# Keys of four sequences multiplied beside the prompt's attention, from early queries, and the other four's spread over the loop

## The reference, cut to what matters

```python
q, k, v, logf, u = project(x, w_in, b_f)                  # D 1024, 8 heads of 64
attn = fox_prompt(q, k, v, logf)                          # 1024 rows, causal, with a decay bias
pool = pool_mix(u_ext, 0, w_pool, pool_scale)
x1   = layer_norm(ALPHA * x + concat(attn, pool) @ w_o)
y    = layer_norm(ALPHA * x1 + (silu(x1 @ w_gate) * (x1 @ w_up)) @ w_down)   # DFF 2816
# the eight sequences: the same, with
s = einsum('bqhd,bkhd->bhqk', q, k_all) * HEAD_DIM ** -0.5 + (F[P:] - F)      # k_all: 4096 cached rows + 1
p = softmax(s);  out = einsum('bhqk,bkhd->bqhd', p, v_all)
```

## Time and profile before

| what | value |
|---|---|
| median of 3 runs | 1494.49 us (1493.03 to 1495.39) |
| profiled execution | 1488.73 us, its span 1486.6 us |
| PE busy | 1371.5 us (92%) |
| DVE busy | 735.6 us (49%) |
| POOL busy | 551.5 us (37%) |
| DMA | 252.91 MB, mean 170 GB/s |
| granted clock of TensorE, mean | 0.960 of full speed |

### The profile page before, as it was taken

The page is one execution under the profiler, slowest core; times in us unless marked ns, Lnnn a source line. Parts: engine busy times, 40 slices in busy tenths (PEclk is TensorE's granted clock), DMA queues, the critical chain, the costliest instruction groups (busy, mean ns, idle before and its releaser), DMA issues.

```text
span 1486.6 us, 21226 instructions
## 1 busy us (share of the span) xinstructions
PE 1371.5 (92%) x7585; PEld 1089.1 (73%) x7585; DVE 735.6 (49%) x1078; ACT 354.7 (24%) x514; POOL 551.5 (37%) x267
## 2 busy tenths in 40 slices
PE   7899999999886989999999999999999999998774
PEld 5898888989686967777767777776777777756421
DVE  4745454453678764455363635564645452325702
ACT  4534353532410232020201120212111112112300
POOL 1110000022135329466457374764665732120500
PEclk9999999999898999999999999999999999999756
DMA  7312011010366437857567577575784863433895
GB/s 254 110 58 67 34 33 68 30 50 1 121 216 200 127 100 243 263 165 236 191 216 246 165 250 249 194 243 169 227 268 154 255 212 113 142 136 127 313 348 212
DMA packets 103176, 252.91 MB, mean 170 GB/s; under 512 B 12576, under 2 KB 13985, under 8 KB 97688
## 3 DMA queue, kind: packets, MB, share of 16 engines
q1 hardware_dynamic: 99776, 240.68, 49.0%
q0 software_dynamic: 3296, 10.88, 2.1%
HBM read 241.89 MB, written 9.86 MB: 169 GB/s over the span
## 4 chain that ended last, share of the span: by engine, by line
PE 79%; DVE 10%; DMA 6%; issue 3%; ACT 2%; SPq 0%; DVEq 0%; ACTq 0%
PE PSM L1271 30%; PE PSM L1289 16%; PE PSM L1041 9%; DMA AR<-ws 4%; PE PSM L1311 4%; PE PSM L1107 4%; PE PSM L1219 4%; PE PSM L1054 3%; PE PSM L1093 2%; PE PSM L1250 1%; DMA WR<-xT 1%; PE PSM L1373 1%; PE PSM L1360 1%; DVE WL L1434 1%; PE PSM L1123 1%
## 5 line engine op out<-in xcount | busy, mean ns | idle before, releaser
L692 POOL TENSOR_TENSOR AR<-AR,QB 128x1024 f32<-128x1024 f32 x128 | 319.0, 2516 | 64.8 <-DMA AR<-cache_k 49.8
L699 POOL TENSOR_TENSOR WL<-WR,WH 128x1024 fp32r<-128x1024 f32 x55 | 133.4, 2426 | 360.7 <-ACT WH L909 360.7
L1271 PE MATMUL PSM<-XH,WH 128*128 128x512 f32 x672 | 215.8, 402 | 0.0
L1271 PE MATMUL PSM<-XH,WL 128*128 128x512 f32 x672 | 211.5, 396 | 0.0
L1271 PE MATMUL PSM<-XL,WH 128*128 128x512 f32 x672 | 211.4, 396 | 0.0
L1611 DVE TENSOR_REDUCE SC<-AR 128x16 f32<-128x1024 f32 x128 | 154.5, 1212 | 105.6 <-POOL AR L692 105.5
L1801 DVE TENSOR_TENSOR ACC<-ACC,PSM 128x512 f32<-128x512 f32 x176 | 119.4, 683 | 131.5 <-PE PSM L1289 131.4
L1271 PEld LDWEIGHTS PSM<-XH,WH 128*128 128x128 f32 x672 | 123.1, 189 | 48.2 <-issue 21.5
L909 ACT CAST WH<-WR 128x1024 fp32r<-128x1024 f32 x55 | 57.5, 1047 | 406.9 <-PE PSM L1271 207.7
L1289 PE MATMUL PSM<-R 128*128 128x512 f32 x528 | 150.6, 394 | 0.0
L1271 PEld LDWEIGHTS PSM<-XH,WL 128*128 128x128 f32 x672 | 126.9, 189 | 30.1
(11 more groups left out here) (245 smaller groups left out, 2125.3 us busy)
## 6 DMA issues: line engine op xcount, KB each, us to landing
AR<-cache_k SPq DMA_DIRECT2D x256, 256.0 KB, 3.4
AR<-cache_v SPq DMA_DIRECT2D x256, 256.0 KB, 3.4
AR<-ws SPq DMA_DIRECT2D x37, 1024.0 KB, 7.0
WR<-ffn SPq DMA_DIRECT2D x66, 512.0 KB, 5.0
WR<-w_in SPq DMA_DIRECT2D x16, 512.0 KB, 4.1
WR<-w_o SPq DMA_DIRECT2D x5, 1024.0 KB, 5.0
WR<-xT SPq DMA_DIRECT2D x8, 512.0 KB, 5.5
AR<-negF_d SPq DMA_DIRECT2D x8, 512.0 KB, 4.1
```

The source lines that it names most:

```text
L692: pool.tensor_tensor(keys, keys, QB[:].rearrange("p (o n) -> p o n", o=1).to_broadcast([P, KP, AW]), ALU.mult).then_inc(k_mul, 1)
L699: pool.tensor_tensor(lo, WR[:, raw_weight(e), :], hi.bitcast(F32), ALU.subtract).then_inc(ffn_lo, 1)
L1271: ins = pe.matmul(out[:, hc], (hi, lo)[a][:, k * P:(k + 1) * P], x[b][:, k, hc], start=(k == 0 and n == 0), stop=(k == KC - 1 and n == 2))
```

## The change

Sequences 0 to 3 (NE = 4, 64 of the 128 key tiles) get their scores in slots 8 to 48 of the attention. Their queries are made by PE in slots 3 and 5 as plain f32 products (32 matmuls of 128 columns), copied by DVE, stored to q_d and spread again. Raw keys go through four tiles that were free then (ACC rows 2 and 3, WR rows 2 and 1), so the raw weights of the prompt's entries from the 15th on use WR row 0 alone. POOL multiplies tile n in slot EMUL[n], DVE sums it in ERED[n], one slot later: three or four tiles in two slots. The scores of a sequence are stored to DRAM (SC_d) and loaded again in the loop. The keys of sequences 4 to 7 are spread evenly over units 2 to 376, one tile in about six units, through a ring of three; their scores stay in AR. The window shrinks from 62 to 56 units, with values at 9, 22, 35 and 48 and the denominator at 12 in place of 8. The tail's constants stay.

```diff
-KS = 4
+KS = 3
+KE = 4
+NE = 4
+EARLY = NE * NKP
-KRED0 = {8: (0,), 9: (1, 2), 10: (3,)} | {n: (n - 7,) for n in range(11, 23)}
-WIN = 62
+WIN = 56
-SPREAD, SUBTRACT, EXPONENT, SUM, DENOM, INVERT = 1, 2, 3, 5, 8, 9
-VALUES = (9, 24, 39, 54)
+SPREAD, SUBTRACT, EXPONENT, SUM, DENOM, INVERT = 1, 2, 3, 5, 12, 14
+VALUES = (9, 22, 35, 48)
-KMUL = tuple(2 + (WIN - 16) * i // (NKP - 1) for i in range(NKP))
-KRED = tuple(o + 3 for o in KMUL)
+LATE = NB * NKP - EARLY
+KMUL = tuple(2 + ((NB - 1) * WIN - 18) * n // (LATE - 1) for n in range(LATE))
+KRED = tuple(u + 3 for u in KMUL)
+EMUL = tuple(8 + n * 40 // EARLY for n in range(EARLY))
+ERED = tuple(x + 1 for x in EMUL)
...
+        KE_SLOTS = [ACC[:, 2, :], ACC[:, 3, :], WR[:, 2, :], WR[:, 1, :]]
+        EARLY_SCORES = [PR[:], PDN[:].rearrange("p a q n -> p (a q n)").rearrange("p (t h) -> p t h", h=H)]
...
+            def early_keys(n):
+                if n >= KE:
+                    pages(n, KE_SLOTS, n % KE, t["cache_k"], ke_ld, k_red, n - KE + 1)
+            def queries(b):
+                if b >= 1:
+                    sp.wait_ge(k_mul, NKP * b)
+                sp.dma_start(QB[:], q_d[b:b + 1, :].to_broadcast([P, AW])).then_inc(qb_ld, 16)
...
+                for n in range(KE, EARLY):
+                    if ERED[n - KE] == x:
+                        if n % NKP == 0:
+                            queries(n // NKP)
+                        early_keys(n)
+                        if n % NKP == KE - 1:
+                            early_scores(n // NKP - 1)
...
+                for n in range(EARLY):
+                    if EMUL[n] == x:
+                        multiply(n)
...
+                for p in (2 * m, 2 * m + 1):
+                    pe.wait_ge(qw_ld[p % 2], 16 * (p // 2 + 1))
+                    for k in range(KC):
+                        ins = pe.matmul(ob[0:NB, (p % 2) * P:(p % 2 + 1) * P], xs_raw[:, k * NB:(k + 1) * NB],
+                                        KE_SLOTS[2 + p % 2][:, k * P:(k + 1) * P], start=(k == 0), stop=(k == KC - 1))
...
+                for n in range(EARLY):
+                    if ERED[n] == x and EMUL.index(EMUL[n]) == n:
+                        reduce_keys(n)
...
-                for c in KRED0.get(n, ()):
-                    reduce_keys(c)
...
+                if b < NE:
+                    dve.wait_ge(sc_ld, 16 * (b + 1))
```

More of the change, by code:

```diff
@@ L418, in build @@
         k_ld = [sem(f"k_ld{n}") for n in range(KS)]
+        ke_ld = [sem(f"ke_ld{n}") for n in range(KE)]
+        qw_ld = [sem("qw_ld0"), sem("qw_ld1")]
+        qw_used, q_st, sc_st, sc_ld = (sem(n) for n in ("qw_used", "q_st", "sc_st", "sc_ld"))
         v_ld = [sem("v_ld0"), sem("v_ld1")]
@@ L451, in entry @@
                 if e >= WS:
-                    sp.wait_ge(ent_lo, e - WS + 1)
+                    before = max(n for n in range(e) if raw_slot(n) == raw_slot(e))
+                    sp.wait_ge(ent_lo, before + 1)
                 if e == 1 or e > KC:
@@ L596, in _ @@
                     continue
-                for i in range(NKP):
-                    n = (b + 1) * NKP + i + KS
-                    if o == KRED[i] + 1 and n < NB * NKP:
+                for n in range(KS, LATE):
+                    if u == KRED[n - KS] + 1:
                         keys(n)
@@ L625, in _ @@
             link = Chain(pool, pool_chain)
-            for tile, value in ((ones, 1.0), (PN, 0.0), (PND, 0.0), (PD, 1.0)):
+            for tile, value in ((ones, 1.0), (PN, 0.0)):
                 pool.memset(tile[:], value).then_inc(consts, 1)
@@ L699, in rest @@
                 pool.tensor_tensor(lo, WR[:, raw_weight(e), :], hi.bitcast(F32), ALU.subtract).then_inc(ffn_lo, 1)
-            for n in range(NKP):
-                multiply(n)
+            pool.wait_ge(sc_st, 16 * NE)
+            for tile, value in ((PND, 0.0), (PD, 1.0)):
+                pool.memset(tile, value).then_inc(consts, 1)
             for e in range(2):
@@ L1446, in key_lo, with reduce_keys @@
                                   ALU.subtract).then_inc(conv_lo, 1)
+            def reduce_keys(n):
+                b, c = divmod(n, NKP)
+                dve.wait_ge(k_mul, n + 1)
+                if n < EARLY:
+                    if c == 0 and b >= 2:
+                        dve.wait_ge(sc_st, 16 * (b - 1))
+                    keys, out = KE_SLOTS[n % KE], EARLY_SCORES[b % 2]
+                else:
+                    if n == EARLY:
+                        dve.wait_ge(sn_st, 16 * 3)
+                    keys, out = KR[(n - EARLY) % KS], scores_of(b)
+                dve.tensor_reduce(out[:, c * KP:(c + 1) * KP, :].rearrange("p j h -> p (j h)"),
+                                  keys.rearrange("p (a n) -> p a n", n=HD), AX.X, ALU.add).then_inc(k_red, 1)
             def mixer_input(g):
@@ L1595, in _ @@
                         entry_lo(KC + n)
+                for n in range(EARLY):
+                    if ERED[n] == x and EMUL.index(EMUL[n]) != n:
+                        reduce_keys(n)
                 if x + 1 in MIXSLOT:
```

226 lines of the change are left out of this document (141 added, 85 removed).

## The result

The changed kernel takes 1511.94 us (median of 8 runs, 1499.53 to 1514.86), the kernel before 1494.51 us beside it (8 runs, 1488.78 to 1498.93). The ratio is 1.0104, 95% interval 1.0079 to 1.0129: slower by about 1%, where the forecast was 1488.5 us and faster. The range (up to 1511) just misses it. The number is that of rival R1, 1511.5 us.

A forecast was written before the change was run, and what follows sets the result against it. PE, busy 92% of the span, was taken to bound the whole. The terms -18 - 7 + 7 + 12 = -6 us, from a median of 1494.5 us, gave 1488.5 us, with a range of 1475 to 1511 us.

The forecast's parts named there:

- R1: Rival, 30%: in the attention DVE and POOL wait for one another and become its bound; (d) +35 us, total 1511.5 us.
- (a): Output stage: sums and multiplications leave it, so DVE is less late for PE; -18 us (-12 to -24).
- (b): Loop: the denominator four units later ends PE's waits for DVE's copies; -7 us (0 to -9).
- (c): Slots 3 and 5: the early queries add 32 f32 matmuls to PE; +7 us (5 to 9).
- (d): Attention: 64 sums on DVE and multiplications on POOL enter and hold each other; +12 us (3 to 35).
- 23 us more for DVE: Attention, in (d): 22 two-operand DVE operations each held 1.05 us by POOL, putting DVE at 182 of 192 us.
- about 3 us of lateness cost PE nothing: Attention, in (d): a slot's results are wanted late in the next slot, so about 3 us of DVE lateness is free.
- 2 x 1.1 us: Slots 17 and 33, in (d): a sum stands ahead of DVE's copy for v_p, for which PE already waits.
- if the clock fell in the attention: Sign that the forecast is wrong altogether: PE's granted clock falls in the attention, where it was 1.00.
- average of 1.05 us: Attention, in (d): wait of a held DVE operation, with POOL busy 85% and half an instruction, 1.2 us, left.
- R2: Rival, 20%: the attention takes it all in, sums filling DVE's rest; (d) 3 to 5 us, total 1479.5 us.
- R3: Rival, 12%: output stage still held by layer norm or a w_o load; (a) -10, sum +2, total 1496.5 us.

The follow-up runs named there:

- experiment 4: Kernel before with only sequence 0's 16 multiplications and sums in the output stage cut small, nothing moved; 1475.4 us, ratio 0.9895.
- experiment 5: Kernel before with only the denominator moved from unit 8 to 12 of the window and its inverse from 9 to 13; 1487.1 us, ratio 0.9963.
- experiment 12: Changed kernel run once more, unchanged, and profiled a second time (span 1510.0 us); 1510.8 us, ratio 1.0119.
- experiment 10: Changed kernel with two early sequences (32 tiles), one tile a slot and none beside low parts, GpSimd waiting for its slot, window 62; 1477.9 us, ratio 0.989.
- experiment 13: As experiment 10, with the two sums ahead of the copy for v_p in slots 17 and 33 moved away; 1473.7 us, ratio 0.9873.
- 7: Changed kernel with one early sequence, its 16 tiles in slots 18 to 25 and 34 to 41, seven sequences in the loop; 1513.9 us, ratio 1.0146.
- 6: Changed kernel with one early sequence in place of four, 16 tiles evenly over slots 8 to 48, seven sequences in the loop; 1522.8 us, ratio 1.0201.
- 9: Changed kernel with one early sequence, one tile a slot and none beside low parts, GpSimd waiting for its slot, window 62; 1475.6 us, ratio 0.9875.
- experiment 1: Changed kernel with POOL's 64 early multiplications cut to 8 of 64 columns of each head row; 1481.3 us, ratio 0.9937.
- experiment 2: Changed kernel with DVE's 64 early sums taken over 4 of 64 columns of a head, multiplications whole; 1497.2 us, ratio 1.0019.
- experiment 11: Changed kernel with its 64 tiles two to a slot in 32 slots clear of low parts, GpSimd waiting for its slot; 1516.7 us, ratio 1.0168.
- experiment 3: Changed kernel with both the early multiplications and the early sums cut small, loads and queries kept; 1470.5 us, ratio 0.9852.

## Why the prediction was wrong, step by step

- **(a), the output stage: right.** -18 was given (-12 to -24), and the stage lost 20.7 us; by itself, in experiment 4, 18.9. From 452.57 on stands one unbroken run of matmuls of 51 us, and what is late next is, as said, the last four row tiles.

```profile
452.57 51.22 PE PSM L1321 x432
```

- **(b), the denominators: right.** -7 was given. All 5.6 us of waits are gone and experiment 5 measures 4.9 us of the loop. The loop of the changed kernel is 8.4 us shorter; where the other 3.5 come from was not separated.
- **(c), the queries: right.** +7 was given, slots 3 and 5 grew by 7.5 us, and slot 8 begins 7.8 us later (7.1 in the second profile).
- **(d), the attention: the step that failed.** +12 was given, 36 to 43 us were measured. The holds were there, 16 us in all where "23 us more for DVE" was the estimate. The step that failed is the one from lateness to time, "about 3 us of lateness cost PE nothing". That is not so in slots 17, 18, 33 and 34, where PE waits for a copy: it already rests there 1.7 to 2.6 us in the kernel before, so there is no slack at all. In slot 17 every microsecond of DVE's lateness was one of PE's, 1.12 in experiment 10 and 4.3 in the changed kernel. It can cost more than once, since the clock often falls behind the longer rest: one sum of 1.2 us in slot 17 made 1.12 us of rest and 2.7 us of time (experiment 10, undone in 13). The prediction named this place ("2 x 1.1 us") with a price two and a half times too small, and priced no clock, which was 15 to 22 us of the loss. It did say that it would be wrong if the clock fell in the attention, where it was 1.00. Outside these places the tolerance did not hold for 64 tiles either: single low parts were held far longer than the average of 1.05 us that the sum took (5.89 us for one of 1.2 in slot 29), and PE then waited for a row minimum. Why ScalarE's copies in slots 11, 27 and 43 came later, 5.1 us in all, was not followed up.
- **The rivals.** R1 had the result: waits in the attention, low parts of 2 us and more (2.41 and 2.00), 1511.5 us. That the number fits so closely is luck: its 35 us for (d) were 36 to 43, and the other stages gave more than its sum had. Its mechanism is half right. DVE and POOL do wait for one another, but no stretch runs at the pair's pace throughout: DVE waits only 8.3 us for multiplications in all (5.2 in the second profile), and slots such as 20, 22, 23 and 35 are no longer than before in either profile. Some 17 of the 36 us sit in slots 16 to 18 and 32 to 34, 7 more in slots 11, 27 and 43, where PE waits anyway; the rest is spread, and more so in the second profile, as R1 would have it. With 16 or 32 tiles that are placed and made to wait for their slot there is no such loss, so R2 ("the attention takes it all in") is right for half the load under that condition; 16 tiles without the wait cost 14 and 21 us (experiments 7 and 6). R3 is refuted by (a).
- **Tail and loop.** I gave the loop nothing but the denominators; it gave 3.5 us more than experiment 5, and the first units another 3. The tail moved between runs, -3.3 and +2.2 us, on the streamed weights.

Summed by the second profile, which is near the median: +7.1 + 43.5 + 2.5 - 20.7 - 2.9 - 8.4 + 2.2 = +23.3 us of span. The medians differ by 17.4 us. The profile of the kernel before is 5.8 us faster than its median; among other things none of its slots 18, 34 and 50 has the slow matmuls that experiment 5 has in all three.

## What to carry to other kernels

"Busy 86 of 192 us" is not room of 106 us. Before work is put beside a stage, list the places at which the bounding engine already rests: there every added microsecond is paid in full and, where the clock falls behind the rest, again in slower matmuls. Everywhere else this stage took 32 sums and 32 multiplications for 1 us; 64 of each it did not take in any of the placings tried. An engine's program says in which order its work runs, not when: GpSimd's multiplications ran ahead of their slots, straight behind a store that had held POOL up, until they were made to wait for the slot. And of a change with several parts, measure each: two were good here, and one of them (the denominator) needs none of the rest. Before a microsecond or two between two profiles is explained, look for the same difference where nothing was changed.

## What I had not expected of the hardware

- That the length of a rest does not decide by itself whether the clock falls. In slots 17 and 33 a rest of 1.7 us left the next matmuls at 0.32 us in all seven profiles that have no sum ahead of the copy (before, 4 to 7, 9 and 13). A rest of 2.84 us in slot 17 put them at 0.49 us in experiment 10 and left them at 0.32 in experiment 1; rests of 3.95 and 6.05 us there (the two profiles of the changed kernel) put them at 0.49. The rest of 2.64 us in slots 18 and 34 left them at 0.32 us in both slots of the kernel before and of experiment 13, and put them at 0.49 in both slots of experiments 5 and 10. What else decides isn't shown here.
- That one low part can be held through more than one multiplication: 1.2 us of work took 5.89 us beside a pair of them (experiment 12, slot 29) and 8.90 in experiment 2, slot 45.
- That two executions of one kernel with the same sum of rests (34.3 and 34.4 us) differ by 7.4 us in the length of the same matmuls. The eight runs of the changed kernel spread over 15 us, those of the kernel before over 10; that the clock makes the wider spread is not shown, and experiment 11, with more loss, spreads over 7.
- That the loads of 64 key tiles beside the attention, 216 GB/s in the row of experiment 3, cost nothing that the traces show. What that kernel lost there lies in slots 17, 18, 33 and 34, and the 3.1 us of slots 18 and 34 came in experiment 5 without them; the small sum in slots 17 and 33 without the loads wasn't tried.
